# An MLP in crossed products: four sums of activation blocks go from VectorE to GpSimd, and low halves change places

## What is computed

```python
def sq_relu_mlp(y, w_up, w_down):
    u = y @ w_up                                # 1024 -> 4096
    return jnp.square(jax.nn.relu(u)) @ w_down  # 4096 -> 1024

h = h + y                                       # y: mLSTM mixer (layer 0), differential attention (layer 1)
h = h + sq_relu_mlp(rmsnorm(h, norm_gains[i, 1]), mlp_w_up[i], mlp_w_down[i])
```

## Time and profile before

| | before |
|---|---|
| median of three runs | 1193.34 us (1193.17 to 1194.18) |
| the profiled execution | 1193.44 us, its span 1191.6 us |
| granted clock of TensorE, mean | 0.997 |
| TensorE busy | 99% |
| VectorE busy | 85% |
| ScalarE busy | 58% |
| GpSimd busy | 10% |

### The profile page before, as it was taken

One profiled execution on the slowest core, in us unless ns is written; L12 is line 12 of the kernel. 1 busy time (PEld: TensorE's weight loads), 2 busy tenths in 40 slices (PEclk: granted clock), 3 DMA queues, 4 the chain that ended last, 5 costly groups with the idle time before them and its releaser, 6 DMA issues.

```text
span 1191.6 us, 22996 instructions
## 1 busy us (share of the span) xinstructions
PE 1176.0 (99%) x8809; PEld 1126.1 (95%) x8809; DVE 1013.5 (85%) x1623; ACT 696.8 (58%) x1201; POOL 113.7 (10%) x171
## 2 busy tenths in 40 slices
PE   9999999999999999999999999999999998999998
PEld 8999999999999999999999999987899988989988
DVE  6889888788899999998568988887898999999973
ACT  6777877745544444535357887876545355444453
POOL 3211110100110110101010000000001001001000
PEclk9999999999999999999999999999999999999999
DMA  7343342433563553673131222223336535446532
GB/s 179 95 110 87 89 111 75 151 105 107 108 143 107 133 121 119 138 206 107 56 105 54 68 59 77 80 70 118 101 134 127 127 117 116 122 124 143 162 105 72
DMA packets 152377, 131.89 MB, mean 111 GB/s; under 512 B 23209, under 2 KB 143073, under 8 KB 152289
## 3 DMA queue, kind: packets, MB, share of 16 engines
q1 hardware_dynamic: 141600, 104.93, 29.8%
q0 software_dynamic: 10560, 25.66, 10.9%
q10 hardware_dynamic: 128, 0.09, 0.0%
HBM read 111.43 MB, written 19.24 MB: 110 GB/s over the span
## 4 chain that ended last, share of the span: by engine, by line
PE 71%; issue 19%; DVE 5%; ACT 2%; DMA 1%; POOL 1%; SPq 0%; DVEq 0%; POOLq 0%; ACTq 0%
PE ps L2335 29%; PE ps L2027 18%; PE ps L2262 17%; PE ps L2553 2%; PE ps L2082 1%; PE ps L2100 1%; ACT hi L741 1%; DVE lo L1611 1%; DVE lof L1604 1%; DVE lo L1618 1%; DMA xin<-in_x_dram 1%; DVE tbuf L1662 1%; PE ps L2214 0%; DVE tbuf L1667 0%; DVE u L1662 0%
## 5 line engine op out<-in xcount | busy, mean ns | idle before, releaser
L2027 PE MATMUL ps<-yh,wh 128*128 128x264 f32 (+1 forms) x704 | 160.5, 302 | 0.0
L741 ACT ACTIVATE hi<-lof 128x1024 fp32r<-128x1024 f32 x80 | 83.4, 1052 | 129.3 <-DVE lof L1604 122.7
L2027 PE MATMUL ps<-yl,wh 128*128 128x264 f32 (+1 forms) x704 | 155.3, 295 | 0.0
L2027 PE MATMUL ps<-yh,wl 128*128 128x264 f32 (+1 forms) x704 | 155.3, 295 | 0.0
L2335 PE MATMUL ps<-th,hi 128*128 128x264 f32 (+1 forms) x448 | 126.8, 283 | 0.1
L2335 PE MATMUL ps<-tl,hi 128*128 128x264 f32 (+1 forms) x448 | 126.4, 282 | 0.0
L2335 PE MATMUL ps<-th,lo 128*128 128x264 f32 (+1 forms) x448 | 126.3, 282 | 0.0
L1611 DVE TENSOR_TENSOR lo<-lof,hi 128x1024 fp32r<-128x1024 f32 x80 | 97.2, 1223 | 25.5 <-ACT hi L741 23.9
L2262 PE MATMUL ps<-ah,hi 128*128 128x264 f32 (+1 forms) x448 | 115.8, 316 | 0.1
L2262 PE MATMUL ps<-al,hi 128*128 128x264 f32 (+1 forms) x448 | 115.6, 316 | 0.0
L2262 PE MATMUL ps<-ah,lo 128*128 128x264 f32 (+1 forms) x448 | 115.3, 315 | 0.0
(11 more groups left out here) (332 smaller groups left out, 3374.8 us busy)
## 6 DMA issues: line engine op xcount, KB each, us to landing
raw<-in_mlp_w_up_dram SPq DMA_DIRECT2D x32, 1024.0 KB, 5.6
raw<-in_mlp_w_down_dram SPq DMA_DIRECT2D x32, 1024.0 KB, 5.0
raw<-in_diff_w_in_dram SPq DMA_DIRECT2D x24, 512.0 KB, 3.7
raw<-in_mlstm_w_in_dram SPq DMA_DIRECT2D x16, 512.0 KB, 4.4
h_sum<-abuf POOLq DMA_DIRECT2D x24, 264.0 KB, 4.7
h_sum<-abuf POOLq DMA_DIRECT2D x24, 256.0 KB, 4.9
h_sum<-h POOLq DMA_DIRECT2D x16, 264.0 KB, 2.4
h<-h_sum POOLq DMA_DIRECT2D x2, 2112.0 KB, 10.3
```

The source lines that it names most:

```text
L741: return nc.scalar.activation(o, i, ACT.Copy, scale=scale)
L2027: last = mm(ps[:, bank + s, 0:w_], w[:, slot, kb, :], m[:, kb, t0:t0 + w_], start=(kb == 0 and n == 0), stop=(kb == CB - 1 and n == 2))
```

## The change

GpSimd makes the four sums, in its list ahead of the DMAs of the group's first plain down pair, after it has waited for the group's last square and last low half. VectorE's block_forms is gone. At pair 5 of the group VectorE makes three of the four weight sums of pair 7 first, then that pair's natural low half, then the low halves of block sums S2, S3 and S1, then the fourth weight sum; A22's low half stands at the head of pair 6. ScalarE rounds S1, A22 and takes the snapshot ahead of pair 7's weight sums, and S2 and S3 behind the copy-out of pair 5 and pair 7's natural high half instead of ahead of them.

```diff
@@ gpsimd
+            def block_forms(layer, i):
+                w = mlp_shape(layer)[1]
+                made = 4 * ((GROUPS - 1) * layer + i // 8)
+                last = 8 * (4 * layer + i // 8) + 8
+                b11, b12, b21, b22 = (blocks_f[:, :, n, 0:w] for n in range(4))
+                pool.wait_ge(sqa_done, last)
+                pool.wait_ge(a_ready, last)
+                nc.gpsimd.tensor_tensor(b22, b22, b12, ALU.subtract).then_inc(b_made, 1)
+                pool.wait_ge(b_made, made + 1)
+                nc.gpsimd.tensor_tensor(b12, b12, b11, ALU.subtract).then_inc(b_made, 1)
+                pool.wait_ge(b_made, made + 2)
+                nc.gpsimd.tensor_tensor(b11, b22, b11, ALU.add).then_inc(b_made, 1)
+                pool.wait_ge(b_made, made + 3)
+                nc.gpsimd.tensor_tensor(b21, b21, b11, ALU.subtract).then_inc(b_made, 1)
@@ residuals, gpsimd
                 for i in range(PAIRS):
+                    if sent_down(i) and i % 8 == 4:
+                        block_forms(layer, i)
                     for m in range(2):
@@ mlp, scalar
                     if first_crossed:
                         block_hi(i, "S1")
+                        block_hi(i, "A22")
+                        snap(i)
                     if crossed(i + 1):
                         form_hi(i + 1, "S23")
-                    if crossed(i):
+                    if crossed(i) and not first_crossed:
                         snap(i)
-                    if first_crossed:
-                        block_hi(i, "A22")
...
-                    if sent_down(i) and i % 8 == 5:
-                        block_hi(i, "S2")
-                        block_hi(i, "S3")
                     if not crossed(i) and not in_tail(layer, i):
...
                     elif layer == 0 and i == PAIRS - 1:
                         split_unit(U_IN1 + 1, 1, 1, 0)
+                    if sent_down(i) and i % 8 == 5:
+                        block_hi(i, "S2")
+                        block_hi(i, "S3")
@@ mlp, vector
                     first_crossed = crossed_down(i) and i % 8 == 6
+                    if first_crossed:
+                        block_lo(i, "A22")
                     if crossed(i + 1):
                         form_lo(i + 1, "S23")
-                    if first_crossed:
-                        block_lo(i, "S1")
...
-                    if first_crossed:
-                        block_lo(i, "A22")
...
-                    if sent_down(i) and i % 8 == 4:
-                        block_forms(i)
-                    elif sent_down(i) and i % 8 == 5:
-                        block_lo(i, "S2")
-                        block_lo(i, "S3")
                     after = crossed(i + 2)
+                    last_plain = sent_down(i) and i % 8 == 5
+                    if last_plain:
+                        form(i + 2, "S1", 0)
+                        form(i + 2, "S3", 0)
+                        form(i + 2, "S2", 1)
                     if after:
                         natural_lo(i + 2, True)
...
-                    if after:
+                    if last_plain:
+                        block_lo(i, "S2")
+                        block_lo(i, "S3")
+                        block_lo(i + 1, "S1")
+                    elif after:
                         form(i + 2, "S1", 0)
                         form(i + 2, "S3", 0)
                     if crossed(i):
                         total(i, "C12")
-                    if after:
+                    if after and not last_plain:
                         form(i + 2, "S2", 1)
```

More of the change, by code:

```diff
@@ L1674, in act_lo @@
                                     ALU.subtract).then_inc(a_ready, 1)
[L1676 to L1688, removed]
                 def block_lo(i, name):
```

## The result

The changed kernel takes 1212.64 us (median of four runs, 1212.34 to 1214.48), the kernel before, on the same chip, 1193.53 (four runs, 1193.17 to 1194.18). The ratio is 1.0161, with a 95% interval of 1.0148 to 1.0174: slower by 19.1 us. The forecast was 1216.1 in a range of 1204 to 1225. The profiled execution took 1214.48, its span is 1212.4 and its mean granted clock 0.989 (before: 1193.44, 1191.6 and 0.997).

What follows compares the result with a forecast made beforehand. VectorE, by setting L, was taken as the bound despite TensorE's 99%. Delays of 10.7 us in layer 1 and 12.1 in layer 0, slow clock included, gave +22.8 on 1193.3: 1216.1 us, range 1204 to 1225.

Steps and rivals of the forecast that it cites:

- L: Start of the first of the four sums on VectorE in each group; claimed VectorE sets it, whatever TensorE does.
- Step (1): VectorE loses four sums per group, 1.22 us each in layer 1 and 1.25 in layer 0: 4.9 or 5.0 us.
- Step (2): GpSimd's price for the four sums: 2.6 us per 1024 columns, 2.65 per 1056, four in 10.6 to 10.9 us.
- Step (3): GpSimd's sums and VectorE's two-SBUF-input instructions take turns: 9.7 us of blocking for 4.9 given away, net +4.7 per group.
- Step (4): New VectorE order behind the sums: TensorE starts S2 at L + 21.0, 2.9 us later behind the hand-over; C11 of pair 15 L + 36.6.
- Step (5): Pair 12's sends and ScalarE's copy of pair 13 come later, at L + 15.4; 1.7 us of cover left, costing nothing.
- The clock: Slow clock behind a third-group stall of 5 us or more adds 1.1 us per layer; its absence, with (b), 0.18.
- (a): No blocking beside GpSimd's sums, VectorE keeps 1.22 us, GpSimd's DMA bounds: 1190.5 us, 1192 at worst; chance 0.11.
- (b): Blocking, but each GpSimd sum 0.3 us shorter, 7.8 us less in all: 1208.3 us; chance 0.18 together with slow clock missing.
- (c): Blocking where VectorE keeps its turn, so sums 3 and 4 run late: 5.8 us more per group, near 1250; chance 0.05.
- (d): Order alone: VectorE let go 5 us sooner, all TensorE stalls (5.9 + 1.1) gone, 1186 us; chance 0.03.

Runs made afterwards that it cites:

- copies: Against the changed kernel, each of GpSimd's four sums became two one-input copies of another block (sums left out of the computation): 1206.8 us, ratio 1.0107.
- fills: Against the changed kernel, each of GpSimd's four sums became two constant fills that read nothing (sums left out of the computation): 1185.36 us, ratio 0.9933.
- the sends first: Against the changed kernel, GpSimd issues the two DMAs of the group's first plain down pair ahead of the four sums: 1232.92 us, ratio 1.0328.
- ScalarE's order alone: Against the kernel before, ScalarE has the new order; sums stay on VectorE, which keeps its old order: 1200.96 us, ratio 1.006.
- the sums alone: Against the kernel before, GpSimd makes the four sums and all else keeps the old order: 1219.15 us, ratio 1.0215.

## Why the prediction was right, and where its sizes were off

**What bounds.** TensorE was busy 99% of the span, yet the argument that VectorE sets L held. L to L in layer 1 went from 86.6 and 84.9 us to 88.5 and 88.4 (898.48 to 987.00, and on to 1075.42, in the rows of the last low half), in layer 0 from 87.0 and 85.6 to 89.6 and 89.1. The forecast said 89 in layer 1.

**Step (1)** stands: 24 sums are gone. **Step (2)**, the price of a sum, is the term that was mis-sized. A free one takes 2.39 us, not 2.6, and 2.46 to 2.48 for 1056 columns, not 2.65: 1.33 us for 528 columns, doubled, was the estimate, and 528 columns more cost only 1.14. A turn of both engines is 3.34 us (990.32 to 993.66) where the step had 3.55. The fourth sum ended at 999.73, L + 10.6, for 11.4. The Trainium skill, "GPSIMD Engine Reference", section 3.1, from which 2.3 was worked out, came nearer than the row of 528 columns did.

**Step (3)** is shown by the runs, and it was the step that decided the sign. Blocking of 8.75 us less the 4.9 given away makes 3.85. The weight sum of 1000.20 shows the same from the other side: it starts at L + 11.1, and before it started 1.2 behind 982.51, at L + 7.25. The step said 4.7 net. Sums of 1212.6, copies of 1206.8 and fills of 1185.4 in the same place of the queue part the causes: it is reading that blocks. The rule of the Trainium skill, "SBUF — State Buffer", "Who interferes with whom", says that a VectorE instruction with two SBUF inputs contends with a GpSimd instruction that reads SBUF and not with one that only writes there; the fills against the copies agree with both halves of it.

**Step (4)**, the order, was right in kind: TensorE waits for S2, never for S1. S2 starts at L + 20.2 for the 21.0 forecast, C11 of pair 14 at L + 25.1 for 26.1, C11 of pair 15 at L + 35.6 for 36.6. All are early by the same 0.8 to 1.0, which is step (2)'s.

**Step (5)** held for the changed kernel. ScalarE's copy of pair 13's first half:

```profile
1003.87 0.60 ACT L759 ACTIVATE abuf<-ps 128x512 f32<-128x512 f32 x1 [0.43 <-DMA h_sum<-abuf]
```

That is L + 14.8 for 15.4, and VectorE has no wait ahead of pair 15's plain low half (1006.76, behind the weight sum of 1006.16). But the 1.7 us of cover were cover only while VectorE was late: in the run with copies VectorE idles 2.46 us ahead of its row of 1002.20, for a high half of ScalarE. And the step missed another such wait: ahead of the natural low half VectorE waits for TensorE, through ScalarE, if it comes early. The changed kernel has it in the first groups (3.55 and 2.43 us), the fills with 4.59, the sends first with 2.45. The working, made on a second group, had no term for it, and it came out since the open wait there replaces a turn of blocking.

**The sum.** Layer 1: L of the second group moved by 1.9 (2.5 forecast), of the third by 3.5 (4.2), TensorE behind the third hand-over by 2.1 (1097.69 is L + 20.2; S1 2.9 later, against 20.97; 2.9 forecast). Layer 0: 2.6 (3.25), 3.5 (4.6) and 2.2 (3.2). That is 15.8 for 20.7, so 4.9 too much, 0.8 in each of six periods. The other way went the clock: behind the third hand-over it cost 2.7 us in either layer, for 1.1 each. 15.8 + 5.4 = 21.2, and the traces are 20.8 apart. So the two errors partly cancelled, 4.9 down and 3.2 up, and that the forecast lies within 3.5 us of the measured time is partly luck.

**The clock.** The term of 1.1 was taken from the one long stall of before, 3.1 us. In the trace after it came to 2.6 or 2.7 behind stalls of 3.0, 5.16 and 3.79 us, to 1.4 behind one of 4.45, and to nothing behind 0.47 and 2.04. The forecast made it hang on a stall of 5 us or more behind the third hand-over. The stalls there were 3.79 and 3.00 us, and it came all the same. So its coming was forecast rightly, its condition and its size were not: one case gives neither. With ScalarE's order alone the slow clock followed a stall of 2.31 us; with the sums alone none followed one of 2.28.

**The rivals.** (a) fell: VectorE didn't keep its 1.22 us. The run with fills comes nearest to what it would be, 1185.4, better than the 1190.5 worked out, but the fills are over in 8.0 us, where four free sums of 2.39 would take about 9.8, an estimate. (b), with sums 0.3 us shorter and 1208.3, was two thirds true in its price (0.2), and the clock took the gain back. (c), VectorE keeping its turn, fell: they alternate one for one. The row that was held against it could not decide, since what VectorE had queued next there takes one input from PSUM, and kept its 0.42 us while GpSimd's select ran to 554.38:

```profile
553.82 0.42 DVE L1662 TENSOR_TENSOR tbuf<-u,ps 128x264 f32<-128x264 f32 x1
```

(d), the order alone with VectorE let go sooner, 1186, was not reached with the sums on either engine; only the fills, which leave the sums out, come to 1185.4. The order with the sums on VectorE gives 1188.9, VectorE's part of it alone 1189.4, and these are the best complete versions of the kernel that the runs found: the change's order without its move of the sums.

## What to carry to other kernels

Before moving work from VectorE to GpSimd, look at what VectorE does meanwhile. If that has two SBUF inputs and the moved work reads SBUF, as here, the move can cost more than it gives: each sum of 1.22 us given away cost 2.2 us of blocking, and VectorE got later by giving work away. When a change has two parts, price them apart: the order was worth -4.6 us, the sums +25.6. And before an idle wait is removed or filled, look at what already lies over it: in the changed kernel part of the blocking was free since VectorE would have waited there, and the queue order with the sends first lost it.

## What the runs showed of the hardware that was not expected

The two engines alternate strictly while both always have an instruction ready, and the wait is inside the duration of the blocked one: sums of 3.27 us for 2.39, low halves of 3.4 for 1.22, copies of 1.91 for 1.05, with no idle time before them. A turn costs VectorE about 2.2 us whether the instruction that it holds takes 0.69 (2.89 in the run with the sends first) or 1.22 (3.42). A fill of 1024 columns takes 0.96 us on GpSimd and doesn't lengthen the low half beside it (1.23 us); a copy takes 1.05 and blocks one for about 0.8. A VectorE instruction with one input from PSUM kept its 0.42 us beside a select of GpSimd (553.82 in the kernel before).

The slow clock lasted 5.8 to 6.1 us behind three of the stalls and 3.0 behind another that was longer than two of the three (4.45). It didn't follow the length of the stall alone. What decides between these the runs leave open.
